# Attention scores from fp32r products over stacked halves, both heads of a pair in one step

## The reference, cut to what matters

```python
GROUP_PATTERNS = ((128, 1), (512, 4), (2048, 16))
def _attention_mixer(hn, w_in, w_out):
    ...
    for g, (window, dilation) in enumerate(GROUP_PATTERNS):
        q = _rope(qkv[:, :, g, 0], cos, sin)
        k = _rope(qkv[:, :, g, 1], cos, sin)
        v = qkv[:, :, g, 2]
        o, lse = _dilated_window_attention(q, k, v, dilation, window // (2 * dilation))
    ...
# inside: each query attends to keys within +-64 positions of its class (tokens p, p+d, p+2d, ...)
    s = jnp.einsum('nhbid,nhbjd->nhbij', qp, kw) * (dh ** -0.5)
    s = jnp.where(valid, s, -jnp.inf)
    m = jnp.max(s, axis=-1, keepdims=True)
    p = jnp.exp(s - m)
    den = jnp.sum(p, axis=-1, keepdims=True)
    o = jnp.einsum('nhbij,nhbjd->nhbid', p, vw) / den
```

## Time and profile before

| | |
|---|---|
| runs of the kernel | 2865.55 us median of 3 (2864.75 to 2868.45) |
| span of the profiled execution | 2864.4 us |
| TensorE busy | 2581.1 us, 90% of the span |
| VectorE, ScalarE, GpSimd busy | 1287.2, 848.1, 797.2 us |
| DMA over the span | mean 104 GB/s |

### The profile page before, as it was taken

The page is one execution under the profiler, slowest core; times in us unless marked ns, Lnnn a source line. Parts: engine busy times, 40 slices in busy tenths (PEclk is TensorE's granted clock), DMA queues, the critical chain, the costliest instruction groups (busy, mean ns, idle before and its releaser), DMA issues. The chain is left out here.

```text
span 2864.4 us, 39052 instructions
## 1 busy us (share of the span) xinstructions
PE 2581.1 (90%) x13832; PEld 2035.0 (71%) x13832; DVE 1287.2 (45%) x2871; ACT 848.1 (30%) x2178; POOL 797.2 (28%) x1303
## 2 busy tenths in 40 slices
PE   5999999999999999999999998898889993267978
PEld 4777777777777777777777776777678873265767
DVE  5333333334444444443344434754322799725434
ACT  4233233332223222223333333323244320014222
POOL 1644444444444444443101110211011110121200
PEclk9999999999999999999999996999999997588989
DMA  4122222222222222222212112876465450384333
GB/s 149 50 58 69 69 69 69 66 64 69 69 69 69 69 62 69 69 62 74 59 50 60 52 41 72 301 254 208 158 206 162 143 151 20 90 239 165 133 138 125
DMA packets 173481, 298.43 MB, mean 104 GB/s; under 512 B 32880, under 2 KB 107632, under 8 KB 170096
## 3 DMA queue, kind: packets, MB, share of 16 engines
q1 hardware_dynamic: 173296, 296.00, 33.4%
HBM read 177.80 MB, written 86.67 MB: 92 GB/s over the span
## 5 line engine op out<-in xcount | busy, mean ns | idle before, releaser
L848 PE MATMUL att_pj<-hT_hi,att_wh 128*128 128x512 f32 (+1 forms) x1728 | 633.7, 367 | 20.7 <-ACT att_val L674 10.6
L848 PE MATMUL att_pj<-hT_lo,att_wh 128*128 128x512 f32 (+1 forms) x1728 | 631.4, 365 | 0.0
L848 PE MATMUL att_pj<-hT_hi,att_wl 128*128 128x512 f32 (+1 forms) x1728 | 630.5, 365 | 0.0
L721 DVE CUSTOM_DVE_ANT_0 att_sm<-att_sc,att_mask 128x256 f32<-128x256 f32 (+2 forms) x480 | 179.9, 375 | 930.5 <-PE att_sc L794 915.6
L642 ACT ACTIVATE att_pr<-att_sm,att_stats 128x256 f32<-128x256 f32 (+2 forms) x480 | 225.7, 470 | 927.1 <-DVE att_stats L721 926.5
L618 POOL TENSOR_TENSOR att_sw<-att_sw,att_rope 128x1280 f32<-128x1280 f32 x48 | 146.2, 3045 | 913.8 <-DMA att_sw<-att_t 913.7
L848 PEld LDWEIGHTS att_pj<-hT_hi,att_wh 128*128 128x128 f32 x1728 | 328.1, 190 | 68.7 <-issue 17.6
L848 PEld LDWEIGHTS att_pj<-hT_hi,att_wl 128*128 128x128 f32 x1728 | 328.0, 190 | 43.6
L848 PEld LDWEIGHTS att_pj<-hT_lo,att_wh 128*128 128x128 f32 x1728 | 328.7, 190 | 41.5
L794 PE MATMUL att_sc<-att_qk 64*128 64x256 f32 (+2 forms) x960 | 302.9, 396 | 4.5 <-DVE att_qk L752 4.5
L816 PE MATMUL att_po<-att_val,att_pt 128*128 128x64 f32 (+1 forms) x1664 | 257.8, 266 | 0.0
(11 more groups left out here) (234 smaller groups left out, 3959.0 us busy)
## 6 DMA issues: line engine op xcount, KB each, us to landing
att_raw<-in_w_att_dram SPq DMA_DIRECT2D x72, 512.0 KB, 3.6
att_sw<-att_t SPq DMA_DIRECT2D x192, 160.0 KB, 2.8
comb_o<-o_scratch SPq DMA_DIRECT2D x60, 256.0 KB, 4.3
o_scratch<-att_o SPq DMA_DIRECT2D x48, 256.0 KB, 3.1
placed_f<-att_place SPq DMA_DIRECT2D x8, 1024.0 KB, 4.5
e_scratch<-att_place SPq DMA_DIRECT2D x8, 1024.0 KB, 4.5
comb_fpre<-placed_f SPq DMA_DIRECT2D x16, 512.0 KB, 5.5
f_scratch<-comb_ft SPq DMA_DIRECT2D x16, 512.0 KB, 4.0
```

The lines of the kernel that those rows point to most:

```text
L721: dve.tensor_tensor_reduce(sm[:, n % 2, 0:w], sc[:, n % 2, 0:w], mask[:, a:a + w], -SCALE, 3e38, ALU.add, ALU.min, st[:, s // 2, h, 0:1]). ...
L848: last = pe.matmul(pj[:, c % 3, 0:n], w[:, which, kt], h[:, kt, lo:lo + n], start=(r == 0), stop=(r == CHUNK_MMS - 1))
```

## The change

Rotated keys and queries are written as fp32r high and low parts. `kh` and `kl` hold one head's 64 rows of high (low) key parts twice, in rows 0 to 63 and 64 to 127; `qs` holds for each head the high part of the queries in one half of the rows and the low part in the other. One product of `qs` with `kh` over 128 rows and one with `kl` give all four products of parts. ScalarE makes the high parts (`keys_hi`, `queries_hi`), VectorE the low ones (`keys_lo`, `queries_lo`), and SyncE copies the second halves (`cross`, eight DMAs an iteration). Both heads of a pair are handled in one step: 10 steps a unit, 12 slots an iteration, 18 projection matmuls in a slot. All windows have one or two whole blocks of 128 keys (no 64-row or 192-column pieces; the keys have 64 zero columns behind them), and the 256 sample tokens are also in class order, so that their tiles in groups 1 and 2 have 128 keys instead of 256. Weight parts have two buffers instead of three. In group 2 the unit's output and its statistics are each stored with ten DMAs instead of three.

```diff
+        if g == 0:
+            out.append((P0 + P * i - 64, 256, "first" if i == 0 else ("last" if i == PT - 1 else "at64"), (i, i + 1)))
         elif g == 1:
-            out.append((P * (i - 1), 256, "at128", [(i - 1, 128, 0), (i, 128, 128)]))
+            even = i - i % 2
+            out.append((P0 + P * even, 256, ("at0", "at128")[i % 2], (even, even + 1)))
         else:
-            out.append((P * i, 128, "class64", [(i, 128, 0)]))
+            out.append((P0 + P * i, 128, "class64", (i,)))
     first = len(value_blocks(g)) - 2
     for i in range(2):
-        mask = ("at0", "at128")[i] if g == 0 else ("mod4" if g == 1 else "mod16")
-        out.append((PROMPT, 256, mask, [(first, 128, 0), (first + 1, 128, 128)]))
+        if g == 0:
+            out.append((S0, 256, ("at0", "at128")[i], (first, first + 1)))
+        else:
+            out.append((S0 + P * i, 128, ("class64", "class16")[g - 1], (first + i,)))
...
-ATT_STEPS = 2 * TILES
-SLOTS = ATT_STEPS + 2
+SLOTS = TILES + 2
...
-        qk = m.sb("qk", [P, 2, 2, TOK])
+        kh = m.sb("kh", [P, 2, COLS], F32R)
+        kl = m.sb("kl", [P, 2, COLS], F32R)
+        qs = m.sb("qs", [P, 2, TOK], F32R)
...
+            def cross(unit, part):
+                lo, hi = PARTS[part]
+                done = 4 * unit + 2 * (part + 1)
+                for tile, ready in ((kh, k_hi), (kl, k_lo)):
+                    sp.wait_ge(ready, done)
+                    sp.dma_start(f(tile[64:128, 0, lo:hi]), f(tile[0:64, 0, lo:hi])).then_inc(crossed[part], 16)
+                    sp.dma_start(f(tile[0:64, 1, lo:hi]), f(tile[64:128, 1, lo:hi])).then_inc(crossed[part], 16)
...
+                    v = dram[PROMPT:TOK].rearrange("(l a b) c -> b l a c", a=2, b=8)
+                    for b in range(8):
+                        sp.dma_start(v[b], sb[16 * b:16 * b + 16, PT:TILES, :]).then_inc(done, 16)
...
+                if proj is not None:
+                    raw_load(3 * proj + V_TILE)
+                    swap(proj, K_TILE)
+                    if proj + 1 < UNITS:
+                        raw_load(3 * (proj + 1) + K_TILE)
+                    swap(proj, Q_TILE)
+                    cross(proj, 0)
+                    if proj + 1 < UNITS:
+                        raw_load(3 * (proj + 1) + Q_TILE)
+                    cross(proj, 1)
...
+                    if 1 <= proj <= POWER_TASKS + 1:
+                        load_seed(proj - 1)
...
+            def keys_hi(unit, part):
+                g = unit // PAIRS
+                act.wait_ge(rope_done, 2 * unit + 1)
+                if unit >= 1:
+                    act.wait_ge(scored, score_count(unit - 1, (PT - 1, TILES - 1)[part]))
+                for h in range(2):
+                    rows = slice(64 * h, 64 * h + 64)
+                    dst, src = part_in_class_order(kh[rows, h], t[rows, 0], g, part)
+                    act.copy(dst, src).then_inc(k_hi, 1)
+            def queries_hi(unit, part):
+                g = unit // PAIRS
+                act.wait_ge(rope_done, 2 * unit + 2)
+                for h in range(2):
+                    rows = slice(64 * h, 64 * h + 64)
+                    dst, src = part_in_class_order(qs[rows, h], t[rows, 1], g, part)
+                    act.copy(dst, src).then_inc(q_hi, 1)
...
                     if proj is not None:
                         for c in range(9):
                             if chunk_slot(c) == s:
                                 chunk_evac(proj, c)
                         if s == 1:
+                            split_hi(3 * proj + Q_TILE)
+                        if s == 5:
                             split_hi(3 * proj + V_TILE)
-                        if proj + 1 < UNITS:
-                            if s == chunk_slot(2) + 2:
-                                split_hi(3 * (proj + 1) + K_TILE)
-                            if s == chunk_slot(5) + 2:
-                                split_hi(3 * (proj + 1) + Q_TILE)
+                        if s == PT:
+                            keys_hi(proj, 0)
+                        if s == TILES:
+                            keys_hi(proj, 1)
+                            queries_hi(proj, 0)
+                            queries_hi(proj, 1)
+                        if s == 9 and proj + 1 < UNITS:
+                            split_hi(3 * (proj + 1) + K_TILE)
+                    if att is not None and s >= 2:
+                        o_evac(att, s - 2)
...
+            def keys_lo(unit, part):
+                g = unit // PAIRS
+                for h in range(2):
+                    rows = slice(64 * h, 64 * h + 64)
+                    dve.wait_ge(k_hi, 4 * unit + 2 * part + h + 1)
+                    dst, src = part_in_class_order(kl[rows, h], t[rows, 0], g, part)
+                    hi, _ = part_in_class_order(kh[rows, h], t[rows, 0], g, part)
+                    dve.tensor_tensor(dst, src, f(hi), ALU.subtract).then_inc(k_lo, 1)
+            def queries_lo(unit, part):
+                g = unit // PAIRS
+                for h in range(2):
+                    rows, other = slice(64 * h, 64 * h + 64), slice(64 - 64 * h, 128 - 64 * h)
+                    dve.wait_ge(q_hi, 4 * unit + 2 * part + h + 1)
+                    dst, src = part_in_class_order(qs[other, h], t[rows, 1], g, part)
+                    hi, _ = part_in_class_order(qs[rows, h], t[rows, 1], g, part)
+                    dve.tensor_tensor(dst, src, f(hi), ALU.subtract).then_inc(q_lo, 1)
...
                         if s == 1:
+                            split_lo(3 * proj + Q_TILE)
+                        if s == 5:
                             split_lo(3 * proj + V_TILE)
                         for which in (K_TILE, Q_TILE):
                             end = chunk_slot(3 * which + 2)
+                            if s == end + 1:
+                                cosine(proj, which)
                             if s == end + 2:
-                                cosine(proj, which)
-                            if s == end + 3:
                                 rotate(proj, which)
-                                if proj + 1 < UNITS:
-                                    split_lo(3 * (proj + 1) + which)
+                        if s == PT:
+                            keys_lo(proj, 0)
+                        if s == TILES:
+                            keys_lo(proj, 1)
+                            queries_lo(proj, 0)
+                            queries_lo(proj, 1)
+                        if s == 9 and proj + 1 < UNITS:
+                            split_lo(3 * (proj + 1) + K_TILE)
...
+            def score(unit, i):
+                n = TILES * unit + i
                 k0, w, _, _ = windows(unit // PAIRS)[i]
-                if s == 0:
-                    pe.wait_ge(rope_done, 2 * (unit + 1))
+                if i in (0, PT):
+                    part = i // PT
+                    pe.wait_ge(crossed[part], 64 * (unit + 1))
+                    if k0 < P0:
+                        pe.wait_ge(crossed[1], 64 * (unit + 1))
+                    pe.wait_ge(q_lo, 4 * unit + 2 * (part + 1))
                 if n >= 2:
-                    pe.wait_ge(masked, n - 1)
-                rows = slice(64 * h, 64 * h + 64)
-                pe.matmul(sc[:, n % 2, 0:w], qk[rows, unit % 2, Q_TILE, i * P:(i + 1) * P],
-                          qk[rows, unit % 2, K_TILE, k0:k0 + w], start=True, stop=True).then_inc(scored, 1)
-            def turn(unit, s):
-                n = ATT_STEPS * unit + s
-                pe.wait_ge(expd, n + 1)
+                    pe.wait_ge(expd, 2 * (n - 1))
+                q0 = query_col(i)
+                for h in range(2):
+                    out, q = sc[:, n % 2, h * w:(h + 1) * w], qs[:, h, q0:q0 + P]
+                    pe.matmul(out, q, kh[:, h, k0:k0 + w], start=True, stop=False)
+                    last = pe.matmul(out, q, kl[:, h, k0:k0 + w], start=False, stop=True)
+                last.then_inc(scored, 1)
...
+            def turn(unit, i):
+                n = TILES * unit + i
+                w = windows(unit // PAIRS)[i][1]
+                pe.wait_ge(expd, 2 * (n + 1))
                 if n >= 2:
                     pe.wait_ge(turn_out, n - 1)
-                for j, (_, k, c0) in enumerate(windows(unit // PAIRS)[s // 2][3]):
-                    last = pe.transpose(tr[0:k, n % 2, j * P:(j + 1) * P], pr[:, n % 2, c0:c0 + k], ident[:])
+                for c in range(0, 2 * w, P):
+                    last = pe.transpose(tr[:, n % 2, c:c + P], pr[:, n % 2, c:c + P], ident[:])
                 last.then_inc(turned, 1)
...
-                    if att is not None and s < ATT_STEPS:
+                    if att is not None and s == 0:
+                        value_turn(att)
+                    if att is not None and s < TILES:
                         score(att, s)
-                    if att is not None and 1 <= s <= ATT_STEPS:
+                    if att is not None and 1 <= s <= TILES:
```

(2 more changed lines are left out.)

261 lines of the change are left out of this document (123 added, 138 removed).

## The result

| | before | after |
|---|---|---|
| runs, median (range) | 2865.74 us (2864.75 to 2868.45, 4 runs) | 2964.68 us (2958.33 to 2973.7, 4 runs) |
| ratio to before, 95% interval | | 1.0347 [1.0327, 1.0366] |
| span of the profiled execution | 2864.4 us | 2964.9 us |
| mean granted clock of TensorE | 0.951 | 0.899 |

The account below looks back on a forecast made before the run. TensorE's issue was taken to bound the kernel. Terms of 19 (iterations 3 to 8), 20 (10 to 16), 24 us (group 2) and the stage's end gave +67 on 2864.4: 2931, with runs 1.2 above, 2933 us; range 2875 to 2985.

Parts of the forecast that it names:

- TensorE's gain: TensorE's own work 60.8, 59.3, 53.8 us an iteration in groups 0, 1, 2, saving 12.3, 14.4, 9.8 us.
- Slot 10: TensorE's wait before tile 8's values, behind Q's rotary work and key subtractions: 3.3, 4.5, 5.6 us (groups 0, 1, 2).
- slot 6: K's cosine in slot 4 delays values in slot 6 by 0.5 us in groups 0 and 1, 2.0 in group 2.
- The end of an iteration: TensorE waits for tile 9's values behind ScalarE's casts, 3.9 us, then at `value_turn`, 0.7: hold 4.6 us every iteration.
- The second part: At an iteration's start `value_turn` waits for c8's evacuation, 0.7 us, where a score covered it before.
- The ring: Loop of late seed, `powers`, K's sine, tile 6 (hold 6.2 us), slot 10: period 76.3 us group 0, 76.6 group 1.
- rival D: GpSimd isn't late, ring's part 6.2 us shorter: groups 0, 1 at 69.2, 68.9 us, total about 2824; chance 0.10.
- The clock: After a hole of 4.4 us TensorE runs 8 matmuls at the lower clock: 1.6 us lost, charged once an iteration.
- rival C: Holes of 4 to 6 us lower the clock three times an iteration, 1.6 us twice more: 3003 us; chance 0.07.
- the iterations that I took as unchanged: Iterations 0, 1, 2, 9 and 17, taken together as unchanged in time.

Follow-up runs that it names:

- e7: e3 with key and large query casts ahead of c7's evacuation, small query casts behind c8's, and the prompt's key parts made in slot 7: 2643.32 us.
- e2: Changed kernel with SyncE storing the last task and loading the next seed right behind Q's exchange, ahead of the key copies: 2964.64 us.
- e1: Changed kernel with ScalarE's output copy right behind the exps of its slot, ahead of the chunk copy and the casts: 2908.58 us.
- e3: Changed kernel with both the edit of e1 and the edit of e2: 2814.25 us.
- e9: Changed kernel with the stacked halves alone undone, scores being fp32 products over each head's 64 rows: 2659.98 us.
- e10: e5 with the second head's score product moved behind the transposes of the tile before: 2800.89 us.
- e5: e3 without the stacked halves: fp32 scores over 64 rows, no key or query parts or copies, each head's scores in its own PSUM bank: 2640.33 us.
- e4: Changed kernel with ScalarE casting high parts of keys and queries in token order in all groups, which changes the computation of groups 1 and 2: 2945.53 us.

## Why the prediction was off by a third, point by point

**TensorE's gain: right.** 60.8 us of own work in group 0, 61.05 measured where nothing else is in the way (e7). Score records stand 0.12 us apart, transposes 0.11 and values 0.10 (I had 0.11):

```profile
507.26 0.28 PE L883 MATMUL att_sc<-att_kh,att_qs 128*128 128x256 f32 x1
507.37 0.28 PE L884 MATMUL att_sc<-att_kl,att_qs 128*128 128x256 f32 x1
```

**Slot 10: the size is right, the victim is another.** Holds of 3.3, 4.5 and 5.6 us were foreseen ahead of tile 8's values; 2.6 to 4.0, 4.8 and 3.6 to 5.6 came, most of it already before the transposes, ended by the exp. In slot 6, where I had 0.5 us (2.0 in group 2), no hole of over 0.6 us stands. VectorE and GpSimd of after at that place:

```profile
988.10 1.49 DVE L804 TENSOR_TENSOR att_t<-att_t,att_rope 128x1280 f32<-128x1280 f32 x1 [4.36 <-DMA att_sw<-att_t]
989.51 6.64 DVE L820 TENSOR_TENSOR att_kl<-att_t,att_kh 64x1024 fp32r<-64x1024 f32 x2
996.18 0.29 DVE L789 CUSTOM_DVE_ANT_0 att_pr<-att_sc,att_mask 128x128 f32<-128x128 f32 x1
```

```profile
988.14 4.25 POOL L664 TENSOR_TENSOR att_sw<-att_sw,att_rope 128x1280 f32<-128x1280 f32 x1 [14.51 <-DMA att_sw<-att_t]
```

The cosine came first and took 1.49, the sine then 4.25 instead of 2.95, and the subtractions behind it 6.64 for two, which is the rest of the sine (2.9) and 1.9 each. I had 3.72 for the cosine and 1.6 for a subtraction: 7.5 us from the landing to the mask, where 8.1 is measured. The two engines exclude each other as before; only who waits has changed. e7 confirms the chain: the subtractions one slot earlier take the hole away in group 0 and leave 1.5 and 1.9 us of it in the others.

**The end of an iteration: mechanism right, size too small where the casts are strided.** 3.9 us foreseen for `values` of tile 9; 4.1 measured in group 0, but 6.6 to 6.9 in groups 1 and 2. The failed term is "1.05 each" for the query casts: it is 1.04 in order and 1.95 strided (those of 256: 0.40 and 0.63, where I had 0.37). The second part, 0.7 us at `value_turn`, is 0.55.

**The ring: the step that failed.** "TensorE reaches them at 37.6: hold 6.2 us" didn't happen; no such hole stands in after, except in iteration 7 with 1.4 us. GpSimd was late, with K's sine straight behind `powers`, but 27.5 to 31.4 us into the iteration and not 37.5 (33.5 in iteration 7; by my own chain that makes 39.8 for the transposes, and they stood at 39.6). In group 0 the seven microseconds are two terms. `powers` took 30.0, not 32.5. And the seed was asked for 2.3 us before the iteration's end, not 2.3 behind it. In group 1, where `powers` took 30.7 to 31.0, it was 4 us before. SyncE of after, iteration 12, which ended at 1018.7:

```profile
1009.76 0.60 SPq L547 DMA_DIRECT2D c_scratch<-att_seed  x1
...
1014.54 0.62 SPq L553 DMA_DIRECT2D att_seed<-in_c_dram  x1
```

and what GpSimd did with it, from the seed's landing to K's sine in iteration 13:

```profile
1017.14 0.53 POOL L628 TENSOR_SCALAR att_seed<-att_seed 128x128 f32<-128x128 f32 x1 [24.74 <-DMA att_seed<-in_c_dram]
...
1047.95 2.96 POOL L664 TENSOR_TENSOR att_sw<-att_sw,att_rope 128x1280 f32<-128x1280 f32 x1
```

From store to load it is 4.78 us, not 6.56. The 6.56 was read rightly from the earlier trace rows, but from one of the two long ones: in 13 of 15 iterations of before it is 5.0 to 5.4 (and `powers` then takes 32.2 us in group 1, not 30.8), as in the iteration of before that starts at 917.36 (timeline of SyncE):

```profile
970.88 0.59 SPq L502 DMA_DIRECT2D c_scratch<-att_seed  x1
...
975.99 0.63 SPq L508 DMA_DIRECT2D att_seed<-in_c_dram  x1
```

And the iteration's end came 13.3 us after c7's (1005.4), not 8.2: the longer hold and the low clock stretch just the part of the iteration which lies behind the seed's start. I had put the hold of one end into the ring without letting it move the iteration's start. e2 shows that the ring isn't on the path in after (0 us), e1 and e3 that it stands right behind it (94 us). So rival D's first words came true, GpSimd wasn't late for TensorE, though SyncE's and GpSimd's part was only some 4 us shorter than I counted and the rest is the iteration that grew. D's 69 us an iteration did not come true: it charged nothing for the clock, and the casts at 4.6.

**The clock: charged once, paid twice.** I took 1.6 us an iteration. TensorE is busy 66.1 us in the iteration of group 0 shown above (66.6 in the mean of iterations 2 to 8), and 61.05 in e7 at clock 1.00, which makes 5.1 us (5.6 in the mean); 59.5 against 54.2 in group 2, 5.3. The starts in iteration 12 account for most of it: eleven 512-column products at 0.43 instead of 0.23 are 2.2 us, and seventeen of 256 columns at 0.21 instead of 0.12 are 1.6, to which values and transposes add. That was the mechanism of rival C, dismissed with 0.07.

**The sum.** With TensorE's own work as foreseen, the measured holes (slot 10, then the iteration's end with `value_turn`) and the clock as the growth of busy time, TensorE's own path closes: 60.8 + 3.2 + 5.0 + clock 5.6 = 74.6 in group 0 (75.2 measured), 59.3 + 4.8 + 7.4 + 4.9 = 76.4 in group 1 (77.1), 53.8 + 4.8 + 7.2 + 5.4 = 71.2 in group 2 (71.7). It must nearly close, since busy and idle time make up the whole; what it tells is the size of each part. In groups 0 and 1 the ring that I counted (76.3 and 76.6) happened to be about as long as that path, so two errors cancelled. In group 2 there is no ring to cancel with: 67.6 foreseen, 71.7 measured, and six times 4.1 is 25 of the 32 us missed. Another 10 lie in the iterations that I took as unchanged, above all 17 with 5.7. The range held the result; of its reason one half was right.

**What I didn't weigh.** I took one head's score at 0.62 us as the price of 64 rows. It is the price of 64 rows with something else in between. That both heads stand in one step would alone have halved it, and the stacked halves' gain over that is only 3.1 us an iteration in group 0 (64.7 against 61.6), for which they bring sixteen operations on ScalarE and VectorE and eight copies. e9 gives the size of this: without them the same change is 208 us faster than before, of which e10 puts some 160 down to the two heads standing side by side.

## What to carry to other kernels

Split a change before you judge it: here one part gained 208 us and the other cost 305 in the same order of work, and after four moves in the queues the version with the costly part was level with the one without it. On an engine that works in order, put the short operation that somebody waits for (a 0.27 us copy) ahead of the long ones which nobody needs yet, and price each hole with the clock behind it. When undoing a suspected cause brings nothing, try it together with the one in front: e2 alone said 0, with e1 it was 94 us.

## What the runs showed of the hardware that I had not expected

- Two fp32 products over rows 0 to 63 and 64 to 127, next to each other and into different PSUM banks, take the time of one: 0.63 us for the pair, 1.26 apart; 160 us in this kernel (e5, e10).
- ScalarE's cast of 64x1024 takes 1.98 us when it reads every fourth element and 1.91 when every sixteenth (after), 1.04 in order (e4).
- Of a GpSimd and a VectorE operation released together either may be the one that waits: the cosine took 3.72 us in the earlier trace rows and 1.49 in after, and the sine 2.95 and 4.25. The longer one was in both cases the one that started later, by 0.58 and by 0.04 us.
- Holes of 3.7 and 1.2 us with a short piece of work between were followed by the lower clock level, just as one of 6.7 us. A single hole of 1.9 us was followed by it in four of six iterations (e7, group 2), and one of 1.5 us in three of seven (e7, group 1). Without holes the granted clock stays at 1.00 for whole iterations (e5, e7).
